# The first two feed-forward tiles made from x that is not yet normed

## The reference, cut to what matters

```
def rmsnorm_2(x, g):
    y = x * lax.rsqrt(jnp.mean(x * x, axis=-1, keepdims=True) + EPS)
    return y * g

def conv_ffn(h, w_up, conv_w, conv_b, w_down):     # D_FF = 2816
    u = h @ w_up                                   # 1024 -> 5632 channels
    u = causal depthwise conv over 3 tokens (u) + conv_b
    gate, val = jnp.split(u, 2, axis=-1)
    return (jax.nn.silu(gate) * val) @ w_down

for i in range(2):
    ...
    x = x + jnp.concatenate([o_mix, o_mem], axis=-1) @ w_out[i]
    x = x + conv_ffn(rmsnorm_2(x, norm_ffn[i]), ffn_w_up[i], ffn_conv_w[i], ffn_conv_b[i], ffn_w_down[i])
```

## Time and profile before

| | |
|---|---|
| median of three runs | 1666.58 us |
| the profiled execution | 1666.89 us |
| its span, first to last instruction | 1665.1 us |
| busy share: PE, DVE, ACT, POOL | 95%, 49%, 42%, 21% |
| mean granted TensorE clock | 0.974 of full |

### The profile page before, as it was taken

How to read it: one execution, slowest core, us unless ns; L and a number is a source line. 1 busy time by engine, 2 the same in 40 slices (tenths; PEclk the granted TensorE clock), 3 DMA queues, 4 the chain that set the end, 5 groups by cost and what they waited for, 6 DMA issues and landing times.

```text
span 1665.1 us, 21113 instructions
## 1 busy us (share of the span) xinstructions
PE 1583.6 (95%) x8546; PEld 1321.6 (79%) x8546; DVE 818.2 (49%) x1325; ACT 699.6 (42%) x1277; POOL 350.6 (21%) x277
## 2 busy tenths in 40 slices
PE   7988998899999999899999999888899999999999
PEld 6777787798887888688888887667787788888887
DVE  5345455657443763554334442457763645335442
ACT  4435445356662433444224343355544434224431
POOL 0000133100330002343104431132202344113420
PEclk9999899999998999999999999988999999999999
DMA  6212111133231002223223331110002223222331
GB/s 220 77 32 82 52 51 65 41 150 102 79 112 51 2 1 82 82 90 120 95 76 101 97 119 54 45 54 14 26 1 89 76 97 112 95 81 97 111 99 56
DMA packets 37313, 128.47 MB, mean 77 GB/s; under 512 B 4176, under 2 KB 8928, under 8 KB 37216
## 3 DMA queue, kind: packets, MB, share of 16 engines
q1 hardware_dynamic: 37216, 127.13, 23.3%
HBM read 125.01 MB, written 2.10 MB: 76 GB/s over the span
## 4 chain that ended last, share of the span: by engine, by line
PE 84%; DVE 7%; ACT 6%; issue 1%; POOL 1%; DMA 0%; POOLq 0%; ACTq 0%; DVEq 0%
PE bank L307 23%; PE bank L309 23%; PE bank L308 23%; PE bank L1069 4%; PE bank L1053 2%; PE bank L1032 2%; ACT whi L288 1%; PE bank L1266 1%; DVE wlo L299 1%; DVE tmp L1799 1%; ACT tmp L1107 1%; PE bank L393 1%; POOL cr L2247 1%; PE bank L1035 1%; PE bank L1038 1%
## 5 line engine op out<-in xcount | busy, mean ns | idle before, releaser
L307 PE MATMUL bank<-hhi,whi 128*128 128x512 f32 (+1 forms) x1072 | 423.3, 395 | 1.0 <-DVE hlo L415 1.0
L309 PE MATMUL bank<-hhi,wlo 128*128 128x512 f32 (+1 forms) x1072 | 419.3, 391 | 0.0
L308 PE MATMUL bank<-hlo,whi 128*128 128x512 f32 (+1 forms) x1072 | 419.2, 391 | 0.0
L299 DVE TENSOR_TENSOR wlo<-wstage,whi 128x1024 fp32r<-128x1024 f32 (+3 forms) x206 | 276.7, 1346 | 158.4 <-ACT whi L288 154.0
L288 ACT CAST whi<-wstage 128x1024 fp32r<-128x1024 f32 (+3 forms) x206 | 229.0, 1116 | 139.8 <-PE bank L309 131.9
L2205 DVE SCALAR_TENSOR_TENSOR cr<-bank,vc,cr 128x511 f32<-128x511 f32 (+1 forms) x176 | 131.6, 749 | 225.3 <-ACT cr L2148 222.1
L307 PEld LDWEIGHTS bank<-hhi,whi 128*128 128x128 f32 (+1 forms) x1072 | 201.6, 188 | 45.7 <-DVE hlo L415 1.2
L309 PEld LDWEIGHTS bank<-hhi,wlo 128*128 128x128 f32 (+1 forms) x1072 | 201.2, 188 | 43.9
L308 PEld LDWEIGHTS bank<-hlo,whi 128*128 128x128 f32 (+1 forms) x1072 | 201.5, 188 | 43.1 <-issue 0.6
L2148 ACT ACTIVATE cr<-bank,vc 128x512 f32<-128x512 f32 x88 | 68.5, 780 | 257.6 <-PE bank L309 254.3
L2247 POOL TENSOR_TENSOR cr<-cr,cr 128x512 f32<-128x512 f32 x44 | 94.5, 2147 | 280.4 <-DVE cr L2205 245.7
(11 more groups left out here) (399 smaller groups left out, 2347.8 us busy)
## 6 DMA issues: line engine op xcount, KB each, us to landing
wstage<-in_wts SPq DMA_DIRECT2D x148, 512.0 KB, 3.5
wstage<-in_wts SPq DMA_DIRECT2D x32, 704.0 KB, 4.0
wstage<-in_wts SPq DMA_DIRECT2D x18, 768.0 KB, 4.4
xT<-in_x SPq DMA_DIRECT2D x4, 512.0 KB, 5.0
xt<-in_x SPq DMA_DIRECT2D x4, 512.0 KB, 5.6
out<-ob SPq DMA_DIRECT2D x8, 256.0 KB, 2.3
U<-in_rel_ext SPq DMA_DIRECT2D x6, 256.0 KB, 9.7
wstage<-in_wts SPq DMA_DIRECT2D x3, 384.0 KB, 3.0
```

Of the source, the lines that this page charges most:

```text
L299: e.tensor_tensor(K.wlo[i % 3][:, 0:w], K.stage[i % 3][:, 0:w], K.whi[i % 3][:, 0:w].bitcast(F32), SUB).then_inc(*K.dve.up(("wlo", i)))
L307: e.matmul(o, lh, rh, start=start, stop=False)
L308: e.matmul(o, lh, rl, start=False, stop=False)
L309: return e.matmul(o, ll, rh, start=False, stop=stop)
```

## The change

During the out steps, each new xT[m] is also multiplied by the gain, without the norm, and split: ScalarE writes `xh` (new line L2110 of the changed kernel) and VectorE `xl` (L2119). TensorE makes gate tile 0 and value tile 0 from xh and xl in step norm1 / norm3, with the sum of the last square between k = 1 and k = 2; `pe_pair` is no longer called in `pe_ffn`. Behind the eight blocks of the norm VectorE multiplies the two banks by `hold` into `xd` (L1836), and the convolutions of these two tiles read xd in place of the bank. The ring for the squares' parts moves to another address.

```
+def pe_norm_first(e, q, K, l):
+    keys = first_pair(l)
+    x = Parts(f"u{l}", *K.xu[l])
+    two = [K.chunk(q, *key) for key in keys]
+    outs = [K.RA.take(q, key) for key in keys]
+    for k in range(8):
+        q.wait_ge(*K.at((x.gen, "hi", k)))
+        q.wait_ge(*K.at((x.gen, "lo", k)))
+        for key, (i, hi, lo), o in zip(keys, two, outs):
+            z = mm3(e, o[:], hi[:, k, :], lo[:, k, :], x.hi[:, k, :], x.lo[:, k, :], k == 0, k == 7)
+            if k == 7:
+                z.then_inc(*K.pe.up(key, K.used(i)))
+        if k == 1:
+            pe_sum_whole(e, q, K, 1 + 2 * l, 7)
+def first_pair(l):
+    return [(f"up{l}", 0), (f"up{l}", 22)]
...
 def dve_norm(...):            # behind the loop over k
+    if pair is not None:
+        for key in first_pair(pair):
+            q.wait_ge(*K.at(first_pair(pair)[1]))
+            e.tensor_tensor(divided(K, pair, key), K.bank(key)[:], K.hold["rb", s][:], MUL).then_inc(
+                *K.dve.up((key, "made"), frees=[key, ("rb", s)]))
...
 def act_out(e, q, K, l):
             act_square(e, q, K, 1 + 2 * l, m, K.sqo[l])
+            e.activation(K.xu[l][0][:, m, :], K.xT[:, m, :], ACT.Identity, scale=K.col("norm_ffn", 8 * l + m)).then_inc(
+                *K.act.up((f"u{l}", "hi", m)))
...
 def dve_out(e, q, K, l):
+    def low(m):
+        hi, lo = K.xu[l]
+        q.wait_ge(*K.at((f"u{l}", "hi", m)))
+        e.scalar_tensor_tensor(out=lo[:, m, :], in0=K.xT[:, m, :], scalar=K.col("norm_ffn", 8 * l + m),
+                               in1=hi[:, m, :].bitcast(F32), op0=MUL, op1=SUB).then_inc(*K.dve.up((f"u{l}", "lo", m)))
...
+            if m:
+                low(m - 1)
+            if m == 7:
+                low(7)
...
 def pe_ffn(e, q, K, l):
-    pe_pair(e, q, K, [(up, 0), (up, 22)], x, 8, T)
...
 conv of ScalarE and VectorE, for these two tiles:
+        q.wait_ge(*K.at((key, "made") if first else key))
+        e.activation(t[:], divided(K, l, key) if first else K.bank(key)[:], ACT.Identity, ...)
+        b, t = divided(K, l, key) if first else K.bank(key), cr[key, "cr"]
...
-        "norm1": lambda: pe_norm(e, q, K, 1), "norm2": lambda: pe_norm(e, q, K, 2),
-        "norm3": lambda: pe_norm(e, q, K, 3), "out0": lambda: pe_out(e, q, K, 0), "out1": lambda: pe_out(e, q, K, 1),
+        "norm1": lambda: pe_norm_first(e, q, K, 0), "norm2": lambda: pe_norm(e, q, K, 2),
+        "norm3": lambda: pe_norm_first(e, q, K, 1), "out0": lambda: pe_out(e, q, K, 0), "out1": lambda: pe_out(e, q, K, 1),
```

More of the change, by code:

```diff
@@ L1782, in pe_norm, with divided @@
     yield
+def pe_norm_first(e, q, K, l):
[12 more added lines that the diff above has]
+            pe_sum_whole(e, q, K, 1 + 2 * l, 7)
+    yield
+def first_pair(l):
+    return [(f"up{l}", 0), (f"up{l}", 22)]
+def divided(K, l, key):
+    return K.xd[:, first_pair(l).index(key), :]
 def act_norm(e, q, K, s, gen):
@@ L1792, in act_norm, with dve_norm @@
     yield
-def dve_norm(e, q, K, s, gen, gname, g0):
+def dve_norm(e, q, K, s, gen, gname, g0, pair=None):
     for k in range(8):
@@ L1799, in dve_norm @@
         e.scalar_tensor_tensor(out=t[:], in0=K.xT[:, k, :], scalar=K.col(gname, g0 + k), in1=K.hold["rb", s][:], op0=MUL,
-                               op1=MUL).then_inc(*K.dve.up((gen, "n", k), frees=[("rb", s)] * (k == 7)))
+                               op1=MUL).then_inc(*K.dve.up((gen, "n", k), frees=[("rb", s)] * (k == 7 and pair is None)))
         if k % 2 == 0:
@@ L2146, in conv @@
         t = cr.take(q, (key, "cr"))
-        q.wait_ge(*K.at(key))
-        e.activation(t[:], K.bank(key)[:], ACT.Identity, scale=K.col(f"cw{l}", 3 * ch + 2), bias=K.col(f"cb{l}", ch)).then_inc(
+        first = key in first_pair(l)
+        q.wait_ge(*K.at((key, "made") if first else key))
+        e.activation(t[:], divided(K, l, key) if first else K.bank(key)[:], ACT.Identity, scale=K.col(f"cw{l}", 3 * ch + 2), bias=K.col(f"cb{l}", ch)).then_inc(
             *K.act.up((key, "c0")))
@@ L2201, in conv @@
     def conv(key, ch):
-        b, t = K.bank(key), cr[key, "cr"]
+        first = key in first_pair(l)
+        b, t = divided(K, l, key) if first else K.bank(key), cr[key, "cr"]
         for s in (1, 2):
+            if first:
+                q.wait_ge(*K.at((key, "made")))
             q.wait_ge(*K.at((key, f"c{s - 1}")))
             e.scalar_tensor_tensor(out=t[:, s:T], in0=b[:, 0:T - s], scalar=K.col(f"cw{l}", 3 * ch + 2 - s), in1=t[:, s:T],
-                                   op0=MUL, op1=ADD).then_inc(*K.dve.up((key, f"c{s}"), frees=[key] * (s == 2)))
+                                   op0=MUL, op1=ADD).then_inc(*K.dve.up((key, f"c{s}"), frees=[key] * (s == 2 and not first)))
     def put(m):
@@ L2786, in dve_program @@
         "group2": lambda: dve_group(e, q, K, 2),
-        "norm1": lambda: dve_norm(e, q, K, 1, "f0", "norm_ffn", 0), "norm2": lambda: dve_norm(e, q, K, 2, "h3", "norm_mix", 8),
-        "norm3": lambda: dve_norm(e, q, K, 3, "f1", "norm_ffn", 8), "out0": lambda: dve_out(e, q, K, 0),
+        "norm1": lambda: dve_norm(e, q, K, 1, "f0", "norm_ffn", 0, 0), "norm2": lambda: dve_norm(e, q, K, 2, "h3", "norm_mix", 8),
+        "norm3": lambda: dve_norm(e, q, K, 3, "f1", "norm_ffn", 8, 1), "out0": lambda: dve_out(e, q, K, 0),
         "out1": lambda: dve_out(e, q, K, 1), "ffn0": lambda: dve_ffn(e, q, K, 0), "ffn1": lambda: dve_ffn(e, q, K, 1)},
@@ L2922, in memory @@
                                      lambda p, i: y["fox", "y", p][:, i, :].rearrange("p (h n) -> p h n", h=2), "o0", y, fox_order())
-            K.sqo = [pairs("sq2", 1, [P, T], s2, [("fox", "pv", 63), ("fox", "fin", 7)])]
+    with above(0) as s:
+        K.sqo = [pairs(f"sq2{l}", 1, [P, T], s, [(n, "pv", 63), (n, "fin", 7)]) for l, n in enumerate(("fox", "mla"))]
+    with above(58880) as s:
+        K.xu = [tuple(sb(f"x{p}", [P, 8, T], F32R, s) for p in "hl")] * 2
+    with above(58880) as s:
+        K.xd = sb("xd", [P, 2, T], scope=s)
     def feed_forward(l):
@@ L2956, in memory @@
                                  lambda p, i: y1["mla", "y", p][:, i, :].rearrange("p (h n) -> p h n", h=2), "o1", y1)
-        K.sqo.append(pairs("sq1", 1, [P, T], s, [("mla", "pv", 63), ("mla", "fin", 7)]))
     K.ff.append(feed_forward(1))
```

## The result

The changed kernel took 1659.63 us (median of 20 runs), the kernel before 1666.59 us beside it. The ratio is 0.9962, with a 95% interval of 0.9955 to 0.9970: 7.0 us faster. The forecast was 1663.0 us in a range of 1659.5 to 1667.0. The direction and the part of the mechanism that moves the pair of tiles were right; the gain is nearly twice the forecast's 3.7 us. The time lies 0.1 us inside the lower end of the range, where the first rival, no fall of the clock, stands (1659.5 to 1659.8). But that rival isn't what happened: the clock did fall, in one layer of two, and part of the gain came from a stretch that the change does not touch. Eighteen of the 20 runs lie between 1657.28 and 1662.78 us, the other two at 1666.73 and 1671.09.

A forecast was written before the change was run, and what follows sets the result against it. TensorE bounds the dense stream, whose start the norm chain holds back. Per layer 3.9 gained - 0.35 (out step) - 1.7 (clock) = 1.85 us, 3.7 for two, giving 1663.0 us; range 1659.5 to 1667.0.

The forecast's parts named there:

- the first rival: TensorE's clock stays full behind the short waits of tile up 1: 1659.5 to 1659.8 us; chance 0.18.
- The pair ahead of the norm: Gate and value tile 0 run before the norm, so tile up 23 starts earlier: gain 3.9 us a layer.
- the 1.51: Delay in us of Ln and the whole norm chain, as the last sum runs behind 12 matmuls of the pair.
- the waits: TensorE in tile up 1 waits 1.4 us ahead of k = 5 and 1.9 us ahead of k = 7.
- Tile 3 of the out step: Its weights come later, as tile 1's xh goes ahead of ScalarE's cast: loss 0.35 us, between 0.1 and 0.7.
- The division and the other parts: Multiplies by hold lie beside ScalarE's cast of up 23, nothing or up to 0.3 us; later convolutions cost nothing.
- The clock: Thin work ahead of up 23 drops TensorE to half clock for 3.4 us: loss 1.7 us a layer, bounds 0 and 3.4.
- The forecast's own case: Clock falls in at least one layer, with 2 to 5.5 us won in all; chance 0.53.
- the sign of being wrong that it named: Full clock through tile up 23, which would give the case without a clock fall.
- Slower: Clock stays low 10.24 us under dense tiles, 5.1 us lost a layer: 1669.8 us; chance 0.05.
- the gain is eaten: Clock low for 6 us and 0.7 us lost at out-step tile 3: 0.6 us won a layer, 1665.5; chance 0.20.
- The pair doesn't run ahead: The pair's k = 0 waits for late xl or weights, sliding the sum; 1 us there gives 1665.0; chance 0.04.

The follow-up runs named there:

- kept busy: Changed kernel plus 5 and 6 useless matmuls in tile up 1, ahead of its waits for k = 5 and k = 7; 1659.51 us, ratio 0.9953.
- layer 1 alone: Layer 0 as in the kernel before, layer 1 as in the changed kernel; 1662.99 us, ratio 0.9979.
- only made: Kernel before, with xh and xl made in both layers but not used, the two tiles run where they ran before; 1667.86 us, ratio 1.0008.
- layer 0 alone: Layer 0 as in the changed kernel, layer 1 as in the kernel before; 1661.61 us, ratio 0.9964.
- late xh: Changed kernel with the xh of tile 1 made behind ScalarE's casts of the weights of tiles 3 and 4; 1662.16 us, ratio 0.9982.
- changed and delayed: Changed kernel with eight useless matmuls added in tile up 9 of layer 0's feed-forward; 1663.15 us, ratio 0.9979.

## Why the prediction was right, and where it was not

*The pair ahead of the norm: right.* Forecast 3.9 us a layer. Up 23 starts 4.00 us earlier after the last square, and the feed-forward from there on costs 0.17 us more where no fall is in it (352.29 against 352.13 in layer 1, and like it in layer 0 of "kept busy"); 0.12 of it lies between the first two matmuls of up 23, which start 0.34 us apart and not 0.227. That is 3.83 net, the whole of layer 1's column and what "layer 1 alone" gave.

*Its pieces were nearly right.* The chain is 1.40 us later, 1.51 forecast; the waits are 1.31 and 1.58 us, 1.4 and 1.9 forecast. One piece of the working doesn't add up: from 677.5, 15 matmuls of 0.227 end at 680.9 and not at 680.6, so the first wait ought to have read 1.1 us; nothing in the gain hangs on it. The step gave the sum behind twelve matmuls as the cause of the 1.51, with the cast "just ahead of Ln". The profile has both ends within 0.02 us of each other (668.96 and 668.98), and "only made", with the sum early, has its Ln only 0.12 us earlier. So the last xl and the cast behind the barrier are as much on the path as the sum: moving the sum alone back would have won 0.1 us. Two things were due at the same moment, and I had credited one.

*Tile 3 of the out step: right.* 0.36 and 0.29 us, 0.35 forecast; it goes when the xh of tile 1 stands behind the cast, as argued.

*The division and the other parts: nothing, as forecast.* The divisions ended at 684.14, the cast at 685.49, and behind 686 us TensorE lost no more than the 0.17 us above where the clock stayed full. The convolutions of these tiles start later and nobody waits for them.

*The clock: the mis-sized term.* Forecast 1.7 us lost a layer. In layer 0 it fell as the row at 1175.40 suggested, for 3.40 us, and cost 1.60; in every profile with the change in layer 0 and nothing added to it (changed, three times; layer 0 alone; and with the delay, where feed-forward 0 grew by 1.81 us for eight matmuls of 0.227). In layer 1 it did not fall, with waits of 1.32 and 1.59 us. I had taken one answer for both layers, since their instructions are the same. The forecast's own case, "a fall in at least one layer", holds, but its sum counted two, and in layer 1 the sign of being wrong that it named, full clock through tile up 23, came true. The fall seems to need both the thin work and the moment, and neither is isolated: it went when the waits were filled, in one profile whose last square stood 380.9 us behind the long fall, where the profiles with a fall have 381.0 to 381.1; and it went in "late xh", with the waits left, at 380.6. The rule of the Trainium skill ("TensorE: Matmul & The Clock Gate", section "HAM oscillation — how this bites in real kernels"), by which waits this short don't slow the clock, agrees with layer 1 and not with layer 0.

*What no step had: the attention stretch.* The prediction held everything outside the change fixed. It was 1.93 us shorter. That this comes from when it is reached, and not from the code of the change, is shown by "changed and delayed" (220.53 with the same code) and by "only made" (218.63 with the pair unmoved). Entries of 751.1 and 754.5 put the first long fall of the stretch at the same place (61.2 to 61.3 us), 753.0 puts it 1.5 us later; why that costs 1.9 us is not shown.

The sum with measured terms: 2 x 3.83 - 0.36 - 0.29 - 1.60 + 1.93 = 7.3 us, 7.0 between the medians. Without the last two errors, 1.6 for layer 1's fall and 1.9 for attention, it is 3.8: the forecast's 3.7. So the distance from the forecast is those two terms, both of the clock. That the measured time lies in the range at all is in part luck: the range has nothing for the attention stretch, and two more medians of the same kernel, 1658.41 and 1658.92, lie below its 1659.5.

*The rivals.* "No fall of the clock" gave the number and not the reason. "Slower" and "the gain is eaten" needed a low clock of 6 us and more over dense tiles; none was seen in a feed-forward. "The pair doesn't run ahead" is excluded by the timeline: no matmul on xh waited.

## What to carry to other kernels

Work that needs no norm can be put in the place where TensorE waits for one. It wins less than its own length where later work still hangs on the norm: here 10.9 us of matmuls moved forward, and up 23 started 4.0 us earlier. Then fill the waits that are left with real work as well (three tiles in place of two: up 23 another 3.6 us earlier in layer 0, and no fall in either profile, though at moments at which the clock might have stayed full anyway). Parts made "beside" other work are on the path where a barrier waits for the last one. And when a kernel alternates dense stretches with thin ones, compare stretch by stretch between instructions that both versions have: a stretch that nobody touched moved by -1.9 to +3.6 us, as much as the edits themselves.

## What the runs showed of the hardware

- TensorE's clock fell to 0.50 for 3.40 us in layer 0 and stayed at 1.00 in layer 1, behind 14.89 us that were alike (11.94 and 11.93 us busy, longest wait 1.58 and 1.59 us). A busy share ahead of a stretch does not tell alone whether the clock falls.
- 3.40 us at half clock under dense 128x512 matmuls cost 1.60 us. With the waits ahead of it filled by eleven matmuls that nobody needs, the same place kept full clock in the one profile taken; it did so too with the waits left, when it was reached 0.4 us earlier, counted from the long fall at 283 us ("late xh").
- In the attention stretch, of fixed work, the last low stretch lasted 3.40 or 13.70 us, and the whole took 218.6 to 224.1 us. Two different kernels with the same places of the low clock took 224.12 and 224.13.
- The full f32 matmul of the sum took 1.02 us, by its two records, between matmuls of the pair (1.14 with the engine idle ahead of it).
